# A two-network forward pass on one core: latent attention's transposes and value products follow its scores by two groups instead of one

## The reference

```python
def hybrid_conv_mla(h, cos, sin, w_in, conv_w, q_norm, kv_norm, w_uq, w_ukv, w_out):
    z = h @ w_in
    ...
    y_conv = gate_b * short_conv(gate_c * u, conv_w)
    q = (rms_norm(cq, q_norm) @ w_uq).reshape(B, S, MLA_HEADS, MLA_NOPE + MLA_ROPE)
    ...
    y_att = mla_attention(q_nope, q_rope, k_nope, k_rope, v).reshape(B, S, MLA_HEADS * MLA_V)
    return jnp.concatenate([y_conv, y_att], axis=-1) @ w_out
```

## Time and profile before

| what | value |
|---|---|
| median of 3 runs | 2191.12 us (2190.85 to 2194.18) |
| the profiled execution | 2203.02 us, its span 2201.2 us |
| TensorE busy | 2139.1 us, 97% |
| VectorE busy | 1481.7 us, 67% |
| ScalarE busy | 1003.4 us, 46% |
| mean DMA rate | 190 GB/s |

### The profile page before, as it was taken

The page is one execution under the profiler, slowest core; times in us unless marked ns, Lnnn a source line. Parts: engine busy times, 40 slices in busy tenths (PEclk is TensorE's granted clock), DMA queues, the critical chain, the costliest instruction groups (busy, mean ns, idle before and its releaser), DMA issues.

```text
span 2201.2 us, 33475 instructions
## 1 busy us (share of the span) xinstructions
PE 2139.1 (97%) x13348; PEld 1911.3 (87%) x13362; DVE 1481.7 (67%) x2077; ACT 1003.4 (46%) x1407; POOL 38.9 (2%) x43
## 2 busy tenths in 40 slices
PE   7999999999999999999999999999999999999998
PEld 5888997888888988888888889888898888988887
DVE  7988868888887646674474458975447546567444
ACT  3433554344434545444354346554445344555343
POOL 0000000000000000000000000000000000001000
PEclk9999999999999979999999999999999999999999
DMA  8887546876886431365545543235554553425552
GB/s 342 307 304 287 197 150 222 311 291 224 310 305 254 148 111 59 116 229 186 182 166 189 175 152 116 77 116 190 183 179 160 185 189 115 154 78 181 181 188 80
DMA packets 75610, 417.53 MB, mean 190 GB/s; under 512 B 5888, under 2 KB 6016, under 8 KB 51840
## 3 DMA queue, kind: packets, MB, share of 16 engines
q1 hardware_dynamic: 75520, 416.27, 52.6%
HBM read 415.20 MB, written 1.05 MB: 189 GB/s over the span
## 4 chain that ended last, share of the span: by engine, by line
PE 88%; DVE 8%; ACT 2%; DMA 1%; issue 1%; SPq 0%; DVEq 0%; ACTq 0%
PE AB L723 13%; PE AB L725 13%; PE AB L724 13%; PE Y L284 9%; PE Y L286 9%; PE Y L285 9%; PE AB L284 3%; PE AB L285 2%; PE AB L286 2%; PE Y L1285 2%; DVE lo L1939 2%; PE M L668 2%; PE N L766 2%; PE Y L723 1%; PE Y L724 1%; PE Y L725 1%
## 5 line engine op out<-in xcount | busy, mean ns | idle before, releaser
L1939 DVE TENSOR_TENSOR lo<-raw,hi 128x2048 fp32r<-128x2048 f32 x310 | 708.3, 2286 | 400.3 <-ACT hi L1428 399.9
L1428 ACT ACTIVATE hi<-raw 128x2048 fp32r<-128x2048 f32 x322 | 615.0, 1913 | 541.7 <-PE Y L286 269.2
L723 PE MATMUL AB<-hi,h_hi 128*128 128x512 f32 x1280 | 506.2, 395 | 0.5 <-DVE lo L1939 0.5
L725 PE MATMUL AB<-hi,h_lo 128*128 128x512 f32 x1280 | 499.1, 390 | 0.0
L724 PE MATMUL AB<-lo,h_hi 128*128 128x512 f32 x1280 | 498.4, 389 | 0.0
L284 PE MATMUL Y<-g_hi,hi 128*128 128x256 f32 x1304 | 369.9, 284 | 0.0
L286 PE MATMUL Y<-g_hi,lo 128*128 128x256 f32 x1304 | 369.5, 283 | 0.0
L285 PE MATMUL Y<-g_lo,hi 128*128 128x256 f32 x1304 | 369.4, 283 | 0.0
L725 PEld LDWEIGHTS AB<-hi,h_lo 128*128 128x128 f32 x1280 | 240.2, 188 | 51.2
L723 PEld LDWEIGHTS AB<-hi,h_hi 128*128 128x128 f32 x1280 | 240.4, 188 | 48.3 <-DVE lo L1939 0.7
L724 PEld LDWEIGHTS AB<-lo,h_hi 128*128 128x128 f32 x1280 | 240.6, 188 | 47.6
(11 more groups left out here) (408 smaller groups left out, 2913.8 us busy)
## 6 DMA issues: line engine op xcount, KB each, us to landing
raw<-slabs SPq DMA_DIRECT2D x322, 1024.0 KB, 5.0
ada_raw<-ada SPq DMA_DIRECT2D x34, 2048.0 KB, 7.8
ada_raw<-ada SPq DMA_DIRECT2D x2, 1024.0 KB, 14.5
kT<-ada SPq DMA_DIRECT2D x1, 1024.0 KB, 10.5
vt<-ada SPq DMA_DIRECT2D x1, 1024.0 KB, 12.6
x<-x_t SPq DMA_DIRECT2D x1, 1024.0 KB, 14.6
out_t<-x SPq DMA_DIRECT2D x4, 256.0 KB, 2.5
vec<-vectors SPq DMA_DIRECT2D x1, 462.0 KB, 3.1
```

Source lines behind the costliest of these rows:

```text
L723: nc.tensor.matmul(out_, h_hi[:, k, at], w_hi, start=start, stop=False)
L725: return nc.tensor.matmul(out_, h_lo[:, k, at], w_hi, start=False, stop=stop)
L1428: nc.scalar.activation(hi[slot][:, :], raw[slot][:, :], ACT.Copy).then_inc(hi_done[slot], 1)
L1939: nc.vector.tensor_tensor(lo[slot][:, :], raw[slot][:, :], hi[slot][:, :].bitcast(F32), ALU.subtract).then_inc(lo_done[slot], 1)
```

## The change

`LAG` is read by the attention loops of TensorE, ScalarE and VectorE, each time for one kind of attention. It is the number of steps between the scores of a group and its transposes; the values come one step behind those. For latent attention it becomes 2. `LEAD`, the pieces beside the steps, the buffers and the order of the slabs stay. TensorE then has nine steps, the last with nothing but the values of group 5, and VectorE's copies and its normalisation of the two batches come a step later than before.

```diff
         LEAD = {"mla": 1, "nsa": 2, "diff": 1}
-        LAG = {"mla": 1, "nsa": 2, "diff": 2}
+        LAG = {"mla": 2, "nsa": 2, "diff": 2}
```

## The result

The changed kernel took 2193.86 us (median of 20 runs, 2192.14 to 2205.52), the kernel before 2190.89 (20 runs, 2189.56 to 2203.11). The ratio is 1.0024 with a 95% interval of 1.0014 to 1.0035. The median lies in the range that was given, but the forecast was no measurable change, and the kernel is slower: the interval leaves out 1, and 0.24% is just over the 0.2% taken as the bound (the interval reaches down to 0.14%). The profiled execution took 2205.52 us, its span 2203.7, against 2203.02 and 2201.2 before.

A forecast was written before the change was run, and what follows sets the result against it. TensorE, busy 2139.1 of 2201.2 us, was taken to bound the kernel. Two new waits, 0.5 + 0.23 = 0.7 us, on the median of 2191.12 gave 2191.8 us, no measurable change, range 2188.5 to 2195.8.

The forecast's parts named there:

- Nothing to gain at the front: Latent attention's scores and transposes: no wait there to remove, so moving transposes away from their exponentials gives and costs nothing.
- First cost, z_lo: Product with slab 10: batch 0's normalisation runs before z_lo on VectorE, so TensorE waits; 0.5 us, bounds 0 and 1.04.
- Second cost, the last values: End of latent attention: the last values wait for the copy of the turned probabilities; 0.23 us, bounds 0 and 0.84.
- Their sum: Both waits in the latent attention, 0.5 + 0.23 = 0.7 us, staying on the path to the end.
- rival 3: Idle around the last values grows, a TensorE clock fall may follow: 1.7 us, time 2193.5; chance 0.04 in deciding size.
- The prediction's own sign of being wrong: First products behind the turn: a granted clock under 1.00 there was listed among the signs of a wrong forecast.
- of another length or at another place: Unplaced clock fall of another length or elsewhere, in either direction, by 1 to 3 us; chance 0.14.
- some 12 us: Whole kernel: the median of the runs shown, 2191.12, was noted as this much less than the profiled execution, 2203.02 us.

The follow-up runs named there:

- e3: Changed kernel with VectorE's batch 0 normalisation moved behind z_lo and the last transposes issued before slab 11's product; 2192.59 us, ratio 1.0011 to the kernel before.
- e11: Repeat: changed kernel with batch 0's normalisation behind z_lo and the last transposes before slab 11's product; 2191.63 us, ratio 1.0005 to the kernel before.
- e10: Changed kernel with only the last transposes moved in front of slab 11's product, the z_lo wait left; 2193.96 us, ratio 1.0015 to the kernel before.
- e2: Changed kernel with only VectorE's batch 0 normalisation moved behind z_lo, the last values still late; 2196.27 us, ratio 1.0018 to the kernel before.
- e1: Changed kernel run again unaltered; 2193.70 us, ratio 1.0018 to the kernel before.
- e4: Changed kernel plus seven matmuls of zeros before the slab wait in the sparse attention's projections; 2194.40 us, ratio 1.0009 to the kernel before.
- e16: Changed kernel run a third time unaltered; 2203.25 us, ratio 1.0035 to the kernel before.
- e8: Changed kernel plus matmuls of zeros around the turn, in the sparse attention's projections and before the modulation's column block; 2193.21 us, ratio 1.0002 to the kernel before.
- e9: Copy of the kernel before, unaltered, run in the place of a changed kernel; 2191.10 us, ratio 0.9997.

## Why the prediction was wrong, and where it was right

- *Nothing to gain at the front:* right. No wait on transposes or scores, and the lag alone costs nothing (e3, e11).
- *First cost, z_lo:* forecast 0.5 us; in the profile 0.26 us idle, and on the path 0.44 us against lag 1, 0.51 against lag 2 without waits (e10). The order on VectorE was as traced out.
- *Second cost, the last values:* forecast 0.23 us; 0.15 us against lag 1 and 0.22 against lag 2 without waits (e2), 0.22 us on top of the first (0.66 - 0.44).
- *Their sum:* forecast 0.7 us, measured 0.66, and it stays on the path: the 439.32 us to the sparse attention are the same before and after.
- *The step that failed* is in rival 3. It set the clock's fall behind the turn aside because "the 2.0 us idle in 317.5 to 320.8 left the clock at 1.00". With the two new waits it fell in each of four profiles (after, e1, e4, e16), and with either wait undone, or the wait around the turn filled, in none. The way that the rival names, idle time around the last values that grows from 2.0 to 2.3 us, is not what the traces show: the wait in front of the turn stayed 1.23 us, and what was new lay ahead of it. The size was priced well in kind, 1.7 us of full speed, of which 0.94 us reach the path. So the fixed cost is 1.6 us and not 0.7. The prediction's own sign of being wrong, a granted clock under 1.00 in the first products behind the turn, came.
- *What was left out altogether* is the long fall in the sparse attention. The forecast held a fall "of another length or at another place" to 1 to 3 us. The profile before had one of 24 us in it, 778 to 804, some 10.8 us of time, which also is most of the "some 12 us" by which the profiled execution lies above the median. I noted that difference and didn't ask for its place. The sum put it at nothing. 16 of 43 executions of the changed kernel have it and 12 of 159 of the kernel before; in the mean that is (0.37 - 0.08) x 10.8 = 3.1 us, more than the 2.5 us by which the main group moved, and it carries the ratio over 0.2%.
- *Luck:* that the median, 2193.86 us, lies in the range is owed to its width; the terms that were added up, 0.7 us, are less than a third of the 3.0 us by which the medians differ.
- *Open:* why the changed kernel falls into it so much more often; of the 2.5 us of the main group, 0.9 us beyond the 1.6 us shown (the falls in the start, the sparse and the differential attention are where executions of one kernel differ, but their frequency was not counted); and whether the fall behind the turn needs both waits, since e2 and e10 have one profile each.

## What to carry to other kernels

Here the transposes did not wait for the exponentials, so a deeper lag had nothing to gain. In such a case look for what the same step moves on the other engines: here a normalisation slid in front of an operation with 0.38 us of slack. Price a new TensorE wait not by its length alone but also by the clock in the work that follows: 0.66 us of new lateness became 1.6, at a wait of unchanged length some 10 us later. And where a profiled execution stands apart from the median, find the place of the difference first, since a change may alter how often it happens; there, seven matmuls of zeros in a wait of 1.6 us left none of 47 executions in the upper group.

## What the runs showed of the hardware that was not expected

TensorE can stay at the lower level while the profile shows no idle time: 22.00 of 22.00 us busy in 782 to 804 at a granted clock of 0.50, behind one wait of 1.62 us; after an almost equally long wait (1.59 us) in another execution it did not fall. The short fall behind the turn (0.19 x 3.3 + 0.29 x 3.7 = 1.7 us of full speed) is as large as that at the modulation's column block before; others are twice as large (e8, 36 to 46: 0.34 x 10 = 3.4 us). And a fall need not cost its size: at the modulation's column block the kernel before has one and e9 has none (granted clock 1.00), yet the way to the residual is 18.84 us in both, and from there to the first gates of the sparse attention 439.32 us in both.
